# Last layer, head 1: ScalarE copies the first piece of turned probabilities before it takes out the projection of a later block

## The reference

```
def block(args):                                     # 128 queries
    rel = einsum('bqhd,bsd->bqhs', iqb, ik)          # indexer: 8 heads of 64
    score = einsum('bqh,bqhs->bqs', iwb, relu(rel))
    score = where(key_pos <= t, score, -inf)
    _, sel = top_k(score, 256)
    ...
    logits = einsum('bqhr,bqkr->bqhk', qb, kv_sel) * R_KV ** -0.5 + bias   # 4 heads, 128 wide
    p = softmax(where(dist >= 0, logits, -inf))
    return einsum('bqhk,bqkr->bqhr', p, kv_sel)
o = einsum('blhr,hrd->blhd', o, w_uv) * silu(z)
mix = concatenate([o_a, o_b]) @ w_out
x = x + gate * rmsnorm(mix, g_post)
```

## Time and profile before

| | |
|---|---|
| time, median of 3 runs | 4081.68 us (4080.99 to 4082.72) |
| profiled execution, its own time | 4079.52 us |
| its span, first to last instruction | 4077.7 us |
| mean granted TensorE clock | 0.983 of full speed |
| busy: PE, DVE, ACT, POOL | 94%, 65%, 33%, 23% of the span |
| last layer, 2870 to 4077 us | PE busy for 1091.38 of 1207.00 us |

### The profile page before, as it was taken

How to read it: one execution, slowest core, us unless ns; L and a number is a source line. 1 busy time by engine, 2 the same in 40 slices (tenths; PEclk the granted TensorE clock), 3 DMA queues, 4 the chain that set the end, 5 groups by cost and what they waited for, 6 DMA issues and landing times. The chain is left out here.

```text
span 4077.7 us, 59823 instructions
## 1 busy us (share of the span) xinstructions
PE 3836.2 (94%) x23331; PEld 2671.9 (66%) x23331; DVE 2645.2 (65%) x4968; ACT 1357.3 (33%) x2906; POOL 920.8 (23%) x543
## 2 busy tenths in 40 slices
PE   8999999998899999997999999998999999998887
PEld 5555556555666666666888888887665656665544
DVE  5666656565777767763555665554466777888884
ACT  1222222222111111111333333332354545665562
POOL 0444334433232223331222222212000000000000
PEclk9999999999999999998999999998999999999998
DMA  7343343432634444433000000003210000000000
GB/s 257 134 151 125 124 151 128 146 109 103 218 132 146 144 148 152 140 117 125 20 27 22 25 24 26 17 15 102 73 37 24 32 24 25 26 19 19 19 3 29
DMA packets 197087, 342.12 MB, mean 84 GB/s; under 512 B 20213, under 2 KB 100426, under 8 KB 196682
## 3 DMA queue, kind: packets, MB, share of 16 engines
q1 hardware_dynamic: 196810, 338.26, 23.9%
HBM read 298.90 MB, written 39.33 MB: 83 GB/s over the span
## 5 line engine op out<-in xcount | busy, mean ns | idle before, releaser
L249 PE MATMUL e_ps<-arena 128*128 128x386 f32 (+1 forms) x1960 | 653.9, 487 | 5.5 <-DVE arena L299 2.9
L249 PEld LDWEIGHTS e_ps<-arena 128*128 128x128 f32 x1960 | 364.8, 191 | 249.9 <-issue 19.1
L249 PE MATMUL o_ps<-arena 128*128 128x320 f32 x1624 | 461.9, 436 | 18.8 <-DVE o_hh L321 5.2
L1726 PE MATMUL d_ps<-hT_in,arena 128*128 128x128 f32 x3072 | 393.7, 283 | 13.3 <-ACT hT_in L1945 11.3
L249 PEld LDWEIGHTS o_ps<-arena 128*128 128x128 f32 x1624 | 301.3, 191 | 147.4 <-issue 13.8
L1726 PEld LDWEIGHTS d_ps<-hT_in,arena 128*128 128x128 f32 x3072 | 360.8, 194 | 28.9 <-ACT hT_in L1945 12.6
L2679 PE MATMUL s_ps<-s_w_out,arena 128*128 128x512 f32 x512 | 243.3, 613 | 0.0
L2484 PE MATMUL s_ps<-hT_in,arena 128*128 128x128 f32 x2016 | 234.2, 275 | 0.0
L2484 PEld LDWEIGHTS s_ps<-hT_in,arena 128*128 128x128 f32 x2016 | 230.4, 192 | 2.4 <-issue 1.4
L1188 PE MATMUL o_ps<-o_w_out,o_gt 128*128 128x512 f32 x512 | 225.0, 598 | 0.0
L640 PE MATMUL e_ps<-e_w_out,e_gt 128*128 128x512 f32 x512 | 223.8, 595 | 0.0
(11 more groups left out here) (524 smaller groups left out, 6890.6 us busy)
## 6 DMA issues: line engine op xcount, KB each, us to landing
arena<-l_w_in SPq DMA_DIRECT2D x48, 1024.0 KB, 7.8
arena<-l_w_in SPq DMA_DIRECT2D x32, 1040.0 KB, 8.4
xb<-x SPq DMA_DIRECT2D x64, 512.0 KB, 4.4
arena<-l_w_in SPq DMA_DIRECT2D x16, 1544.0 KB, 9.1
arena<-l_w_in SPq DMA_DIRECT2D x16, 1280.0 KB, 7.7
arena<-l_w_in SPq DMA_DIRECT2D x32, 504.0 KB, 7.0
arena<-l_w_in SPq DMA_DIRECT2D x16, 768.0 KB, 7.0
o_scratch<-w_ada SPq DMA_DIRECT2D x16, 768.0 KB
```

The costliest lines, as they stand in the source:

```text
L249: m = pe.matmul(bank[(g + k) % 2][:, 0:self.n], rows[:, kk * P:(kk + 1) * P], cols[:, kk, :], start=(kk == 0 and k in (0, 1, 4)), stop=(kk ...
L1726: m = pe.matmul(bank[c % 2][:, t * P:(t + 1) * P], W_in[:, k, (4 * c + t) * P:(4 * c + t + 1) * P], hT[:, k * P:(k + 1) * P], start=(k == ...
```

## The change

In head 1, ACT's calls of `project(i + 2, 0)` and `project(i + 2, 1)` move from ahead of the first copy of turned probabilities to behind it, and ahead of the search rounds. No instruction is added, removed or resized, no transfer is touched, and the orders of PE, DVE, POOL and SP are the same as before.

```
--- before.py
+++ after.py
@@ -2870,9 +2870,6 @@
                     act.wait_ge(*mx_ready.upto(i, h + 1))
                     act.activation(Lg[:, h % 2, 0:(i + 1) * P], Lg[:, h % 2, 0:(i + 1) * P], ACT.Exp, bias=mx[:, h:h + 1],
                                    accum_out=psum_[:, h:h + 1]).then_inc(*exp_ready.inc())
-                    if h == 1:
-                        project(i + 2, 0)
-                        project(i + 2, 1)
                     if h == 3:
                         project(i + 2, 2)
                     for c, (a, w) in enumerate(key_chunks(i)):
@@ -2883,6 +2880,9 @@
                             act.wait_ge(*pv_made.upto(i, n - 3))
                         act.activation(pT[:, n % 4, 0:w // P, :], by_head[6 + n % 2][:, 0:w // P, :], ACT.Copy)\
                            .then_inc(*pt_ready.inc())
+                        if h == 1 and c == 0:
+                            project(i + 2, 0)
+                            project(i + 2, 1)
                         if FIRST_TOPK <= i + 1 < BLOCKS and SHARES[h][1]:
 
                             if c == (n_pieces - 1 if h == 0 else (n_pieces - 1) // 2):
```

## The result

The changed kernel takes 4088.71 us in the median of 20 runs (4084.5 to 4090.37), the kernel before 4082.1 in as many (4078.91 to 4087.38): ratio 1.0015, interval [1.0009, 1.0021]. It is slower by some 6.6 us and not by 0.9, and the time lies outside the range.

What follows compares the result with a forecast made beforehand. It took the DVE-ACT threshold search, with PE behind it, as the bound. Losses of 2.39 us in blocks 1 to 9 less gains of 1.16 and 0.33 gave +0.90 on 4081.68: 4082.6 us, range 4079 to 4087.

Steps and rivals of the forecast that it cites:

- What bounds the layer: Last layer: the threshold search between DVE and ACT has no slack and holds PE's second copy in head 1.
- merged wait: Head 1, block 5: PE's first wait for a copy goes into the second, 1.94 us instead of 1.08.
- ACT's detour: Head 1: ACT waits for the transposes, losing about 0.75 us less its wait for DVE; blocks 1 to 9 sum to +2.39.
- Block 0: No search there, so the gain of the earlier copy stays: -1.16 us.
- Blocks 10 and 11: Logits of piece 2 come 0.4 us earlier, so DVE's search rounds start sooner: -0.11 and -0.22 us.
- Their sum: All blocks together: 2.39 - 1.16 - 0.33 = +0.90 us.
- the clock falls in the longer wait: Rival: head 1's longer PE wait halves the granted clock (a fall), 1.8 us each, up to 4091.6 us; chance 0.02.
- What the profile would show: Heads 1 and 2: ACT's wait for DVE gone, copy waits down some 4 us, block 5's DVE wait 0.92 to 1.15.
- The test that I gave for being wrong: Wrong if head 1's second copy waits do not grow, or block lengths change by over 1 us outside block 0.

Runs made afterwards that it cites:

- the filled kernel: The changed kernel, with PE computing the values of piece 0 of head 1 twice more in blocks 4 to 7, ahead of its wait for piece 1's copy: 4082.88 us.
- second trace of before: The kernel before, unchanged, run and traced once more: 4082.99 us.
- split order of ACT: The changed kernel, but the projection's first three ACT instructions stay ahead of the first copy and the rest follows it; run alone: 4084.78 us.
- fills of blocks 11 and 12: The kernel before, with seven matmuls whose result nobody reads in PE's wait in the scores of each of blocks 11 and 12: 4078.67 us.
- changed again: The changed kernel, unaltered, run and traced once more: 4088.1 us.

## Why the prediction was wrong, point by point

- *What bounds the layer:* right. In head 1 the search chain holds the second copy, and the saved wait went into it. The merged wait was undersized: 1.94 by the sum, 2.22 measured, 2.57 in block 4. In block 5 the second multiplication starts 0.25 later, but PE is done with what stands ahead of it 0.89 earlier and not 0.63: without a wait the first multiplication overlaps the transposes ahead of it, and its row takes 1.06 and not 1.16.
- *ACT's detour:* right. 0.75 us for the transposes; blocks 1 to 3 late by 0.36, 0.51 and 0.56 for 0.33, 0.49 and 0.55; blocks 8 and 9 by 0.27 and 0.07 for 0.25 and 0.08. Block 4 was late by 0.66 and not 0.39: ACT's search round starts there 0.35 us after the start of the projection's last instruction, for 0.11 in blocks 1 to 3, 5 and 6. Nothing in the traces says why.
- *Block 0:* right, -1.03 to -1.06 for -1.16 where no fall covers it. *Blocks 10 and 11:* -0.11 as forecast in block 10. In block 11 PE comes to the scores 0.22 earlier (56.94 us after the block's start for 57.16), as forecast; the block's whole length can't show it, since by the fall in its scores it moves by up to 0.27 in the kernel before itself.
- *Their sum:* the filled kernel, which has all of this and no fall behind the waits for copies, is 0.9 us over before on the same chip. The forecast was +0.90. That it fits so closely is luck: the interval goes from -1.2 to +6, and the terms as measured add up to +1.4, since block 4 lost 0.27 more and block 0 gained 0.13 less.
- *The step that failed* is the clock. The sum takes the lengths of the instructions as they were, which puts the clock's term at nothing, and the rival "the clock falls in the longer wait" got 0.02. I dismissed it because "the wait that the change makes is shorter than that one", the wait of 3.07 us in block 6 behind which the trace had 2.4 GHz. One instance without a fall was read as a safe length. The second trace of before has a fall behind the very same wait, and merged waits of 1.9 to 2.6 us brought one in 11 of 16 blocks. Its price was roughly right: the rival had 1.8 us for a fall, the projection is 1.62 longer (5.36 for 3.74), and a block 1.05 to 1.5, since later waits for ACT give a part back (block 5's wait in head 2 falls from 0.59 to 0.32, and block 7's of 0.67 is gone).
- *The size:* 4088.7 - 4082.9 = 5.8 us of the loss go when the four merged waits are filled; the rest of the 6.6 is the lateness of about 1 us. How the 5.8 come about is shown in part only. Four falls would be 5.1, but the two traces of the changed kernel have two and three of them, 2.9 and 3.8 us. They are 6.0 and 5.3 longer than the trace of the filled kernel, and most of what is left stands in the scores of block 6 (2.6 and 1.1) and in blocks 8 and 9 (0.9 and 1.6), behind waits that the filled kernel has too, in its one trace without a fall.
- *What the profile would show:* ACT's missing wait came as said, and the waits for copies fell by 2.2 us for some 4. DVE's wait in head 2 of block 5 was to grow from 0.92 to 1.15 and is 1.84:

```profile
3185.79 0.15 DVE L2992 TENSOR_SCALAR s_mid<-s_nmid 128x1 f32<-128x1 f32 x1 [1.84 <-ACT s_nmid L2841]
```

ACT's answer is 0.25 late, as the sum has it, but DVE is also done 0.67 earlier with the logits, which PE makes earlier; this the prediction left out. The test that I gave for being wrong, blocks longer by over 1 us outside block 0, is what the table shows.

What stays open: why block 4 is 0.3 later than its terms; whether the early copy has a part in the falls of block 9; why filling the merged waits takes away more than the falls behind them; and what decides in one execution which waits of some 2 us bring a fall.

## What to carry to other kernels

Where an edit turns two short waits of PE into one long one, the sum of idle time is not the price: ask what the granted clock will be behind the longer wait, and look at more than one execution before calling a length of wait harmless. Busy time of PE that grows with the same instructions is the sign on the page. If the wait can't be shortened, work that nobody needs, put inside it and free of the chain, can cost nothing and hold the clock. Here 17 spare matmuls, two repeated products in each of four blocks and the split order of ACT were together worth 0.12% over the kernel before; how much of it each gave was not measured apart, but for the fills of blocks 11 and 12, at 3.1 us with an interval that reaches no change.

## What the runs showed of the hardware

- The granted clock fell behind merged waits of PE of 1.91 to 2.57 us in 11 of 16 cases, and behind the wait of 3.07 us in one of the two traces of before and not in the other. In block 0 it fell behind waits of 1.55 to 1.77 us, in eight traces. The Trainium skill, page "TensorE: Matmul & The Clock Gate", Part 1, calls the number of slow matmuls at the start of a kernel "run-variable". The two traces of before show the like in its middle: falls in blocks 0, 6 and 10 in the one, in none of blocks 0 to 10 in the other.
- Eight scores took 3.79 us at 1.2 GHz for 1.99 at 2.4, and 32 matmuls of 128 columns 5.36 for 3.74. The 32 don't take twice as long because only a part of them lies in the fall. Block 5's, in windows of PE alone (busy PE, granted clock, DMA):

```profile
3184.60:3186.00 1.40, 1.40 (x13) 0.83 0.00 0
3186.00:3187.40 1.40, 1.40 (x9) 0.50 0.00 0
...
3189.40:3190.00 0.60, 0.60 (x7) 1.00 0.00 0
```
- Repeating a closed product in the same PSUM region, 16 matmul records in 1.95 us, did not lengthen the block by itself: block 5 is 0.26 longer with it (filled) and 0.23 without it and without a fall (changed again).
